# A two-layer block on one core: context's output product by blocks in the first expert layer, and all of x's first tiles beside its picks

## The reference, cut to what matters

```python
y, yc = mla_conv_mixer(h, hc, ...)              # x attends to ctx and x; ctx to itself
x  = x  + mod[2] * y ;  xc = xc + modc[2] * yc
h2 = modulate(rms_norm(x, norm2_g[l]), mod[3], mod[4])      # likewise for ctx
x  = x  + mod[5] * peer_ffn(h2, w_q, sub_keys, u, v)

# peer_ffn, 8 heads: queries, two score tables of 128, top 16 of each,
# top 16 of the 16 x 16 sums -> 16 expert rows per token and head
q = (x @ w_q) ; s = einsum('nhpd,hpkd->nhpk', q, sub_keys)
act = gelu(einsum('nd,nhkd->nhk', xb, u[eb]))
out = einsum('nhk,nhkd->nd', gate * act, v[eb])
```

## Time and profile before

| | us |
|---|---|
| median of 3 runs | 2543.28 (2542.82 to 2547.66) |
| the profiled execution, its own time | 2544.54 |
| its span | 2542.5 |
| PE busy | 1966.6 (77%) |
| DVE busy | 1671.9 (66%) |
| ACT busy | 1160.0 (46%) |
| POOL busy | 885.4 (35%) |
| gathers' queue | 847.30 MB of 954.32 MB, 79.9% of the DMA time |
| granted TensorE clock, mean | 0.859 |

### The profile page before, as it was taken

One profiled execution on the slowest core, in us unless ns is written; L12 is line 12 of the kernel. 1 busy time (PEld: TensorE's weight loads), 2 busy tenths in 40 slices (PEclk: granted clock), 3 DMA queues, 4 the chain that ended last, 5 costly groups with the idle time before them and its releaser, 6 DMA issues. The chain is left out here.

```text
span 2542.5 us, 31830 instructions
## 1 busy us (share of the span) xinstructions
PE 1966.6 (77%) x10908; PEld 942.4 (37%) x10908; DVE 1671.9 (66%) x4157; ACT 1160.0 (46%) x3157; POOL 885.4 (35%) x808
## 2 busy tenths in 40 slices
PE   8999887878786767777777776889997676666766
PEld 5667432443341212333333331568752221122110
DVE  1634689887667667767586857473557666666655
ACT  2342456776545444544354534412335444444444
POOL 0001344545434444434343434200115444444342
PEclk8999998888997878888988888899998877788676
DMA  9554999999999999999999999795169999999997
GB/s 365 207 191 134 423 422 418 399 403 414 425 425 426 426 426 426 426 425 426 425 414 426 414 426 426 291 369 186 64 239 411 426 426 426 426 426 426 427 426 306
DMA packets 146995, 954.32 MB, mean 375 GB/s; under 512 B 16529, under 2 KB 22161, under 8 KB 45329
## 3 DMA queue, kind: packets, MB, share of 16 engines
q0 software_dynamic: 113472, 847.30, 79.9%
q1 hardware_dynamic: 33360, 104.98, 11.2%
HBM read 951.17 MB, written 1.05 MB: 375 GB/s over the span
## 5 line engine op out<-in xcount | busy, mean ns | idle before, releaser
L1079 PE MATMUL pY<-uv,diag 64*64 64x512 f32 x6144 | 994.2, 741 | 500.7 <-ACT diag L1155 476.2
L960 POOL DMA_INDIRECT uv<-uv_dram,idx x768 | 860.5, 1120 | 1288.0 <-PE pY L1079 1037.7
L1313 DVE SCALAR_TENSOR_TENSOR uv<-uv,H 128x1024 f32<-128x1024 f32 x768 | 940.0, 1224 | 545.2 <-DMA uv<-uv_dram,idx 526.2
L1079 PEld LDWEIGHTS pY<-uv,diag 64*64 64x64 f32 x6144 | 194.3, 152 | 1128.3 <-ACT diag L1155 977.3
L1147 ACT ACTIVATE gelu<-dots 128x1 f32<-128x1 f32 x768 | 154.8, 202 | 867.3 <-DVE uv L1313 856.9
L1155 ACT ACTIVATE diag<-cst,coef 128x128 f32<-128x128 f32 x768 | 308.3, 401 | 70.9 <-ACT coef L1151 0.4
L1151 ACT ACTIVATE coef<-gelu,gate 128x1 f32<-128x1 f32 x768 | 226.3, 295 | 28.4 <-ACT gelu L1147 0.7
L983 PE MATMUL pqs<-hT,wring 128*128 128x256 f32 x512 | 127.4, 405 | 0.7 <-ACT S L1130 0.7
L983 PEld LDWEIGHTS pqs<-hT,wring 128*128 128x128 f32 x512 | 101.0, 202 | 43.6 <-issue 29.5
L134 PE MATMUL plh<-hT,wring 128*128 128x256 f32 (+1 forms) x512 | 101.7, 360 | 8.8 <-DMA wring<-hg_zz_dram 6.2
L1147 ACT ACT_TABLE_LOAD x79 | 101.4, 1283 | 1.4
(11 more groups left out here) (448 smaller groups left out, 2246.6 us busy)
## 6 DMA issues: line engine op xcount, KB each, us to landing
aw<-ada_w_dram POOLq DMA_DIRECT2D x12, 2048.0 KB, 8.8
wring<-peer_q_dram SPq DMA_DIRECT2D x36, 512.0 KB, 10.3
uv<-uv_dram,idx POOLq DMA_INDIRECT x768
wring<-hg_zz_dram SPq DMA_DIRECT2D x24, 512.0 KB, 8.9
wring<-w_in_dram SPq DMA_DIRECT2D x16, 512.0 KB, 9.6
arena<-hg_zz_dram SPq DMA_DIRECT2D x16, 512.0 KB
arena<-ada_w_dram POOLq DMA_DIRECT2D x4, 2048.0 KB
h_aw<-ada_w_dram POOLq DMA_DIRECT2D x4, 2048.0 KB
```

The costliest lines, as they stand in the source:

```text
L960: nc.gpsimd.indirect_dma_start(out=uv[:, n % SLOTS, :], out_offset=None, in_=t[f"uv{l}"], in_offset=bass.IndirectOffsetOnAxis(ap=idx[:, s ...
L1079: last = nc.tensor.matmul(pY[crossed(own, half), b, half * 512:(half + 1) * 512], diag[own, n % DIAGS, own], uv[own, n % SLOTS, D + half * ...
L1313: v.scalar_tensor_tensor(out=uv[:, j, 0:D], in0=uv[:, j, 0:D], scalar=1.0, in1=H2[:, own, :], op0=ALU.mult, op1=ALU.mult, accum_out=dots[: ...
```

## The change

- The front no longer does x's latent tiles, and no longer ctx's output product, residual and second norm. `modulate(14)` moves into the last step pair of the loop, `modulate(15)` and its turn behind the transposes of O.
- A new class `ContextOutput` opens layer 0's expert phase: w_out's tiles 0 to 3 from the ring, 4 to 7 from the last two slots of `uv`, each block of 128 columns by itself; block 0's sums, norm, queries and scores come between the tiles of block 1.
- VectorE does `topk(0)` before the picks and cuts `topk(1)` and `topk(2)` into step 0, two parts a pick; queries and scores of head 1 go to picks 1, 3 and 6. `keep_warm` ahead of the picks: 3, not 9.
- x's mixer does all 12 tiles beside the picks, three matmuls a pick from pick 4 on; the first two loads (`sync_first`) wait for block 1's sums. LAT, QK_AT, V_AT move by 2, UNIT by 1, CONV from 23 to 31 with 9 taps in 7 picks.

```diff
 front_phase, TensorE
-                def fill(n):
-                    if u < len(UNITS):
-                        x = 2 * u + n
-                        tile(1, x // KT, [x % KT])
-                if u < len(UNITS) and u % 2 == 0:
+                if u % 2 == 0:
                     modulate(6 + u // 2)
...
-            (tiles of w_out, sums of squares, modulate(14))
             modulate(15)
             turn(14)
             turn(15)
 front_phase, ScalarE
                 a.activation(mixc[:, 4 + i, :], convc[:, i, :], ACT.Silu, ...)
-            (squares, take_rows(14), root)
             take_rows(15)
 peer_phase, SP
-            if opening:
-                opening.sync_queries(sp)
+            opening.sync_queries(sp)
+            if l == 0:
+                sides[0].sync_first(sp)
             for h in range(HEADS_AHEAD, HEADS_AHEAD + 2):
                 weights(h)
 peer_phase, VectorE
-            for s in range(1 if opening else AHEAD):
-                for part in range(TOPK):
-                    topk(s, part)
+            opening.vector(dve)
+            for part in range(TOPK):
+                topk(0, part)
+            opening.second(dve)
+class ContextOutput:
+    def tensor(self, pe):
+        products(0, range(KT))
+        products(1, range(RING))
+        sums(0)
+        queries(0, self.pq)
+        scores(0)
+        products(1, range(RING, KT))
+        rows(0)
+        sums(1)
+        queries(1, self.pt)
+        rows(1)
+        scores(1)
+    def vector(self, dve):
+        self.residual(dve, 0)
+        self.norm(dve, 0)
+        self.residual(dve, 1)
+        dve.wait_ge(self.x, 2 * KT)
+        dve.sem_inc(self.acc_free, RING)
+    def second(self, dve):
+        self.norm(dve, 1)
 TargetMixer
-    START, LAT, QK_AT, V_AT, UNIT, CONV, OT, LN, OUT, NORM, TURN = 3, 26, 37, 53, 60, 23, 130, 130, 143, 197, 211
+    START, LAT, QK_AT, V_AT, UNIT, CONV, OT, LN, OUT, NORM, TURN = 4, 28, 39, 55, 61, 31, 130, 130, 143, 197, 211
+        for i in range(2, 2 * self.PAIRS):
+            if n == self.START + -(-8 * (i - 1) // 3):
+                sp.wait_ge(self.x_used, i - 1)
+                self.rest_load(sp, i)
```

More of the change, by code:

```diff
@@ L338, in _ @@
                 load_tile(sp, "w_in", i, first[0] + i)
[L339 to L343, removed]
+            lin_ahead(sp, 1)
         @block.gpsimd
@@ L392, in sums, with tile @@
                 last.then_inc(n_sum, 1)
[L394 to L402, removed]
-                        pe.wait_ge(n_ha if k % 2 == 0 else n_hv, k // 2 + 1)
[L404 to L418, removed]
+            def tile(g):
+                pe.wait_ge(w_loaded[g % RING], 16 * (g // RING + 1))
+                if g % 2 == 0:
+                    pe.wait_ge(acc_free, g + 2)
+                for k in range(KT):
+                    if g == 0:
+                        pe.wait_ge(n_ha if k % 2 == 0 else n_hv, k // 2 + 1)
+                    last = mm(pl[g // 2 % 2][:, g % 2, :], wring[:, g % RING, k * P:(k + 1) * P], h1[:, k, :],
+                              start=(k == 0), stop=(k == KT - 1), skip_group_check=True)
+                last.then_inc(acc_ready, 1)
             def pair(p):
-                tile(0, 2 * p, whole)
-                tile(0, 2 * p + 1, whole)
+                tile(2 * p)
+                tile(2 * p + 1)
             pe.wait_ge(s_zero, 3)
@@ L536, in _ @@
                     last.then_inc(o_t, 1)
[L537 to L550, removed]
             modulate(15)
@@ L664, in _ @@
                                  scale=mx[:, 6 + v % 2:7 + v % 2]).then_inc(at["norm"], 1)
-                if u < len(UNITS) and u % 2 == 1:
+                if u % 2 == 1:
                     take_rows(6 + u // 2)
-                for p in range(LATENT):
-                    if done_at[p] + 1 == u:
-                        take(1, p)
                 if u == 13:
@@ L792, in _ @@
                 v.tensor_tensor(convc[:, i, :], convc[:, i, :], rs[:, CX], ALU.mult).then_inc(c_step, 1)
[L794 to L811, removed]
-                v.tensor_tensor(hT[:, k, CX], xT[:, k, CX], rs[:, XX], ALU.mult).then_inc(r_y, 1)
-            dve.wait_ge(r_y, KT)
-            for k in range(1, KT, 2):
-                own = hT[:, k, CX]
-                v.tensor_scalar(own, own, gainT[:, 0, 1, k, 1:2], modT[:, 0, 3, k, 1:2], ALU.mult, ALU.add)
             dve.wait_ge(m_turned, GROUPS)
+            mod_finish(fin, 0, (2, 3, 4, 5), pc[:, 32:96].rearrange("p (n c) -> p n c", c=2))
             mod_finish(fin, 1, (0, 1), pc[:, 96:128].rearrange("p (n c) -> p n c", c=2))
@@ L954, in _ @@
                     pool.wait_ge(s_top, (s + 1) * LINKS)
-                if opening and n == SLOTS - 2:
+                if n == SLOTS - 2:
                     pool.wait_ge(opening.b1_out, 1)
@@ L1059, in _ @@
                     late = h + HEADS_AHEAD == HEADS
-                    if (b, k) == ((1, 2) if late else (0, 9 if opening and s == 0 else 4)):
+                    if (b, k) == ((1, 2) if late else (0, 9 if s == 0 else 4)):
                         queries(h + HEADS_AHEAD, 0)
@@ L1925, in tensor @@
                     pe.wait_ge(self.x_taken, p - 1)
-            for k in (k0, k0 + 1):
-                last = mm(self.pairs[p % 2][:, i % 2, :], self.H2[:, i % 2, k * P:(k + 1) * P], self.Kx[:, k, :],
-                          start=(k == 0), stop=(k == KT - 1))
-            if k0 == KT - 2:
+            last = mm(self.pairs[p % 2][:, i % 2, :], self.H2[:, i % 2, k * P:(k + 1) * P], self.Kx[:, k, :],
+                      start=(k == 0), stop=(k == KT - 1))
+            if k == KT - 1:
                 last.then_inc(self.x_used, 1)
```

347 lines of the change are left out of this document (204 added, 143 removed).

## The result

Against 2544.7 us of before on the same chip the changed kernel took 2568.2 us (2564.4 to 2574.3, 4 runs): ratio 1.0094, 95% interval [1.0077, 1.0111], or +23.6 us where +10.7 were forecast. The profiled execution is the slowest of the four (2574.3 us, span 2572.5), so its trace has some 6 us that the median has not. The step between the layers (last dot product of layer 0 to first of layer 1) takes 270.7 us in it, 266.5 in the trace of before.

The account below looks back on a forecast made before the run. It took layer 0's stream of 768 gathers at about 426 GB/s as the bound. First gather +4.5, bytes +5.2 and VectorE +1.0 gave +10.7 on 2543.3, so 2554.0 us, range 2545 to 2563 (8 in 10).

Parts of the forecast that it names:

- 1a: Front's attention loop: removed fillers and lower clock net zero (bounds -3 and +4); the added modulate(14) costs +1.4 us.
- The sentence on the gate: TensorE's clock: halves after idling, returns after sustained work, so removing loop fillers costs clock; pointed to the range's upper part.
- 1b: Front's tail: modulation copy, turn, keep_warm(4) at 3.7 us and phase switch; output product starts at 195.1, 12.4 us later.
- 1c: Opening, from output product through block 0's norm, queries, scores and top-k: first gather at 249.0 against 244.5, +4.5 us.
- Rival D: Opening: block order saves nothing because topk(0) stands behind residual(1); otherwise gather 7.6 us sooner, 2546.4 us; chance 0.03.
- 2, bytes: Loads beside the gathers: x's tiles and head 2's loads add 2.23 MB behind the first gather, +5.2 us.
- Cadence: x's tiles beside the picks: one per 2.67 picks, one late by 4 to 7 us, covered by queued gathers.
- Rival B: x's tiles land late: 27 us of TensorE waits, about 10 covered by queued gathers; 2571 us, chance 0.12.
- 3, VectorE: VectorE beside the picks: denser taps where it is full (picks 39 to 64), +1 us, bounds -4 and +5.

Follow-up runs that it names:

- the dummies: Changed kernel with 32 matmuls of 256 columns, results unused, put back into the front's attention loop where the fillers stood: ratio 1.0060 to before.
- picks first: Changed kernel with block 1's last four residuals moved behind topk(0) on VectorE: ratio 1.0085 to before.
- tiles with dummies: Kernel before, old opening, with all 12 x tiles beside the picks, the changed timetable, and unused matmuls where the loop's fillers stood: ratio 0.9983.
- the timetable alone: Kernel before with only the new start numbers and rate of taps for x's mixer, run twice: ratios 0.9985 and 0.9969.
- Tiles alone: Kernel before, old opening, with 12 x tiles beside the picks, their new timetable and no fillers in the attention loop: ratio 1.0022.
- After with four buffers: Changed kernel with four buffers instead of two for x's tiles, four loads going out ahead of the picks: ratio 1.0025 to before.
- the opening alone: Changed kernel with x's four latent tiles back in the front's loop as fillers and x's mixer on its old eight-tile timetable: ratio 1.0045 to before.

## Why the prediction was wrong

The sign and the mechanisms of the opening were right; the size was not, and 2568.2 us lies outside 2545 to 2563. Two steps failed. The queued gathers were to cover a late tile for nothing, and the stream lost 12.1 us. The clock was put at a net of zero in the loop and at full in `keep_warm(4)`, and it cost 6.6 us ahead of the product. A third, the timetable's effect on VectorE, had the wrong sign and hid part of both.

- **1a failed in its size.** "I put the two at zero together; the bounds are -3 and +4." The loop's last scaling of O starts at 185.5 for 180.0, +5.4 where I had +1.4: the whole upper bound. The fillers were cover, as I said, and cover was what kept the clock. The sentence on the gate (Trainium skill, TensorE: Matmul & The Clock Gate, Part 1: The HAM clock gate) had this sign and I left it for the range's edge; the trace agrees with it, 0.79 for 0.91, and the dummies show the cause, since they do nothing but keep TensorE busy.
- **1b failed in the same term.** `keep_warm(4)` was priced by a row at full clock, 3.7 us, and took 6.0; the turn ahead of it 1.86 for 1.0. Product at 201.7 for 195.1.
- **1c was right.** From the product's start to the first gather 54.4 us for 53.9, no point of it more than 1.3 off: late tiles 0.5, queries at half clock 6.35, MAX8 7.3 us behind S. So the first gather's +11.6 for +4.5 is all of the loop and tail. Rival D's mechanism, that the order costs 7 us of gather, is shown too (picks first: 7.2 us); what those 7 us are worth in the kernel's time its ratio can't tell.
- **2, bytes: right as far as it can be seen.** Head 2's keys and tiles went out at 267.6, behind the first gather. The traces show the forecast's 2.23 MB exactly (577.55 to 579.78 MB). What they cost in time was never measured by itself; tiles with dummies (0.9983) against the timetable alone (0.9969, 0.9985) bound the four tiles to a few us.
- **Cadence was the costliest step that failed**: "the gathers queued cover that, as they covered the 8.5". The wait itself came where I had it and at the size I gave it (4 to 7 us; 7.1); the cover was priced by the one case in which it had held. I count the gathers issued less the dot products begun. Before, the 8.5 us wait began 16 us behind the first gather, with 7 in the queue; the gap that it made between two gathers was 12.5 us, and next to nothing was lost. After, at 20, 28 and 36 us there are 5, 4 and 5. 41 us behind the first gather 17 are issued, as forecast, but 12 dot products have begun, where I had put pick 9. At 44 us the 7.1 us wait begins, with 4 in the queue; it runs down to 1, stays at 1 or 2 for 21 us, and before it has filled, the second wait comes.
- Two runs separate the level from the wait. Tiles alone, with the same table and two buffers behind the old opening, has 5 to 7 in the queue from 20 to 90 us; its 6.6 us wait begins with 5, it never falls under 3, and the stretch keeps 420 GB/s. After with four buffers, behind the new opening, has no such wait and keeps a level of 4 or 5 from 20 to 80 us (3 for half a microsecond in all), with 422 GB/s. So neither the new opening's lower level nor the late tiles starved the stream by themselves; together they did, in after as in the opening alone. That the second top-k and head 1's queries beside the first picks set the lower level is read from the order of the instructions; no kernel took them out one by one.
- **Rival B**, given 0.12, was this step's mechanism in part: tiles late, bandwidth under 400. It had 27 us of waits with 10 covered; the 120 us behind the first gather have 15.9 us of waits for x's tiles and 12.1 us lost. That its 2571 lies near 2568.2 is luck: it had neither the clock nor the timetable's gain.
- **3, VectorE, had the wrong sign.** +1 forecast, -9.0 by the trace in x's attention, -4 and -8 us in the two runs of the timetable alone; the lower bound had been -4, for just this case. Which of its numbers does it wasn't tried.

Against the forecast's terms, then: first gather +7.1 more (6.6 of it ahead of the product), the starved picks +12.1, x's attention -10.0 (-9.0 for +1). That is 9.2 of the 12.9 us by which the median's excess was missed; 3.7 stay unplaced. The later, thinner stretches of layer 0 would fill them.

## What to carry to other kernels

Price a wait by the level of the queue that covers it at that moment, not by the longest one that it ever covered: here the same wait of 6.6 us cost almost nothing with 5 gathers queued, and thinned the stream to 339 GB/s where an earlier wait had left 3. Matmuls that fill waits are not free to remove because they are off the path: what they fill may be what holds the clock of everything on it. And when a change carries a new timetable with it, try the timetable alone; here it was the only part shown to pay.

## What the runs showed of the hardware that was not expected

- Adding 32 matmuls to a loop on whose path they don't lie made its pair 10.3 us for 11.4, by the granted clock (0.89 for 0.79).
- `keep_warm(4)`, four 512-column matmuls ahead of the product, runs at half clock itself: 5.8 to 6.2 us in the eight kernels that have it ahead of the new opening, with the product behind it at full clock (7.38 us in each); without it that product takes 9.88. It moves most of the price rather than saving it.
- A 512 KB tile issued at 290.2 us behind two others and a head's keys, beside four or five queued gathers, was used at 307.4: 17 us. Before's slowest took 17.7, also behind two tiles and a head's keys, its earliest 8.1. With four buffers, the tile issued at 244.9, ahead of the first gather, landed after 3.5.
- The step between the layers, which none of the kernels changes, took between 266.5 us (clock at half for 17 us) and 275.6 (31 us) in the fourteen profiled executions: the clock's chance there is larger than most effects measured here.
